# One front stage for vectors, modulation and column turns, and two expert slots filled during routing, in a one-core two-block network

## The reference

```python
mod = silu(c) @ w_mod + b_mod                    # c: one vector; shift, scale, gate for mixer and ffn
u   = rmsnorm(x, norm_mix_g) * (1 + sc_m) + sh_m      # 512 latent tokens
uc  = rmsnorm(ctx, norm_mix_g) * (1 + sc_c) + sh_c    # 256 context tokens, from silu(c_ctx) @ w_mod
y   = gated_deltanet(u, uc, w_in, conv_w, ...)        # projects u and uc first
...
aff = softmax(u2 @ w_router); gates, idx = top_k(aff.T, 64)   # 16 experts, 64 tokens each
hid = silu(xs @ w_gate) * (xs @ w_up); ys = hid @ w_down * gates   # 1024 -> 2048 -> 1024 per expert
```

## Time and profile before

| | us |
|---|---|
| median of 3 runs (lowest, highest) | 2763.99 (2762.11, 2767.11) |
| the profiled execution | 2771.04 |
| its span, first to last instruction | 2769.3 |
| front, start to the first instruction of `gdn_projection` | 74.46 |
| experts, first load issued to last piece landed | 930.5 to about 1898 |
| PE busy in the whole span | 2342.0 (85%) |

### The profile page before, as it was taken

How to read it: one execution, slowest core, us unless ns; L and a number is a source line. 1 busy time by engine, 2 the same in 40 slices (tenths; PEclk the granted TensorE clock), 3 DMA queues, 4 the chain that set the end, 5 groups by cost and what they waited for, 6 DMA issues and landing times. The chain is left out here.

```text
span 2769.3 us, 29918 instructions
## 1 busy us (share of the span) xinstructions
PE 2342.0 (85%) x11740; PEld 1515.1 (55%) x11740; DVE 1005.3 (36%) x1791; ACT 570.2 (21%) x1201; POOL 253.9 (9%) x347
## 2 busy tenths in 40 slices
PE   4999998189985688888888888885998989799998
PEld 2777668179944433333333333332775667687776
DVE  2576515525635101011010101103753554464443
ACT  2442214044401100000000000001232331223311
POOL 2233325820000000000000000000000000000000
PEclk7999988589996899999999999998998999899999
DMA  5123735334330599999999999994421022222030
GB/s 209 47 63 111 226 130 175 64 96 129 91 118 2 225 415 416 417 417 418 418 417 416 416 417 418 417 418 191 164 77 46 31 99 76 86 89 75 31 129 31
DMA packets 209191, 569.88 MB, mean 206 GB/s; under 512 B 62553, under 2 KB 97346, under 8 KB 175682
## 3 DMA queue, kind: packets, MB, share of 16 engines
q1 hardware_dynamic: 206296, 559.97, 53.3%
q0 software_dynamic: 2496, 8.40, 0.9%
q10 hardware_dynamic: 297, 0.11, 0.0%
HBM read 540.14 MB, written 28.31 MB: 205 GB/s over the span
## 5 line engine op out<-in xcount | busy, mean ns | idle before, releaser
L1808 PE MATMUL ps_gate_up<-expert_ring,one_expert_columns 128*64 128x512 f32 x1024 | 488.6, 635 | 143.7 <-DMA expert_ring<-in_moe_w_up_dram 136.2
L1809 PE MATMUL ps_gate_up<-expert_ring,one_expert_columns 128*64 128x512 f32 x1024 | 490.1, 636 | 0.0
L1808 PEld LDWEIGHTS ps_gate_up<-expert_ring,one_expert_columns 128*64 128x64 f32 x1024 | 144.6, 146 | 454.7 <-issue 454.7
L1875 DVE TENSOR_TENSOR hidden_tokens<-silu_gate,ps_gate_up 64x512 f32<-64x512 f32 x64 | 42.4, 690 | 623.3 <-ACT silu_gate L1854 622.8
L1788 PE MATMUL ps_down<-expert_ring,hidden_columns 128*64 128x512 f32 x512 | 226.6, 595 | 0.0
L1789 PE MATMUL ps_down<-expert_ring,hidden_columns 128*64 128x512 f32 x512 | 226.6, 595 | 0.0
L1809 PEld LDWEIGHTS ps_gate_up<-expert_ring,one_expert_columns 128*64 128x64 f32 x1024 | 144.6, 146 | 0.0
L1788 PEld LDWEIGHTS ps_down<-expert_ring,hidden_columns 128*64 128x64 f32 x512 | 67.5, 137 | 130.1 <-issue 127.9
L809 DVE SCALAR_TENSOR_TENSOR conv_out<-conv_in,tap_columns,conv_out 128x770 f32<-128x770 f32 (+1 forms) x96 | 124.4, 1295 | 3.4
L114 DVE TENSOR_TENSOR stream_low<-stream_raw,stream_high 128x2048 fp32r<-128x2048 f32 x48 | 110.0, 2293 | 1.6
L120 PE MATMUL even_bank<-stream_high,columns_high 128*128 128x512 f32 x256 | 107.7, 421 | 2.8 <-DVE columns_low L2377 2.8
(11 more groups left out here) (493 smaller groups left out, 4241.4 us busy)
## 6 DMA issues: line engine op xcount, KB each, us to landing
expert_ring<-in_moe_w_gate_dram SPq DMA_DIRECT2D x64, 2048.0 KB, 18.0
expert_ring<-in_moe_w_up_dram SPq DMA_DIRECT2D x64, 2048.0 KB, 22.5
expert_ring<-in_moe_w_down_dram SPq DMA_DIRECT2D x64, 2048.0 KB, 19.5
win_ring<-in_gdn_w_in_dram SPq DMA_DIRECT2D x16, 1024.0 KB, 6.7
late_mod_ring<-in_w_mod_dram SPq DMA_DIRECT2D x16, 1024.0 KB, 6.1
stream_raw<-in_w_in_even_dram SPq DMA_DIRECT2D x16, 1024.0 KB, 5.3
stream_raw<-in_w_in_odd_dram SPq DMA_DIRECT2D x16, 1024.0 KB, 5.2
stream_raw<-in_w_ple_gate_dram SPq DMA_DIRECT2D x8, 1024.0 KB, 5.0
```

Of the source, the lines that this page charges most:

```text
L1808: mm(psA[LO, c], xe[:, e, k], gu[:, s0, j, cols], start=(k == 0), stop=(k == KC - 1))
L1809: last = mm(psA[HI, c], xe[:, e, k], gu[:, s1, j, cols], start=(k == 0), stop=(k == KC - 1))
L1875: nc.vector.tensor_tensor(hid[HI, c % 2], sg[HI, c % 2], psA[HI, c], ALU.mult).then_inc(hidden, 1)
```

## The change

The four front blocks become one, `front`. SP issues the constants, the context, `x`, all four pieces of `w_mod` and the projection's first weights in one stream, each with its own semaphore. The tokens of context and latent are normalised in place and turned into columns without scale and shift, in two halves between PE's products with `w_mod`; ACT copies them plainly into one wide tile (`columns_wide`), and only when scale and shift are known does ACT apply them, SBUF to SBUF. DVE splits off the high part of all 768 columns and the low part of the latent 512; POOL takes the low part of the 256 context columns, a job that DVE had. In the experts, slots 0 and 1 of the ring are a tile of their own (`expert_ring_early`) that SP fills at the start of `route`; the load loop begins with piece 2, runs over 7 pairs and is followed by the 22 loads of the last pair. `gated` in `route` now lies over the normalised tokens, with a wait for their split into high and low.

```diff
+def front(nc, dram, per, U, spare, junk, loads):
...
+                sp.dma_start(per["ident_ones"][:, :, :], dram["gdn_const"][:, 0:2 * P].rearrange("p (a b) -> p a b", a=2)).then_inc(const_in, 16)
+                sp.dma_start(ctx[:, :, :], dram["ctx"].rearrange("b (t p) d -> p (b t) d", p=P)).then_inc(ctx_in, 16)
+                sp.dma_start(h[:, :, :], dram["x"].rearrange("b (t p) d -> p (b t) d", p=P)).then_inc(x_in, 16)
+                for i in range(PIECES):
+                    sp.dma_start(piece[i], w[:, :, i * COLS:(i + 1) * COLS]).then_inc(slot[i], 16)
+                sp.dma_start(per["gdn_const"][:, :], dram["gdn_const"]).then_inc(fetched, 16)
+                for dst, src in loads:
+                    sp.dma_start(dst, src).then_inc(fetched, 16)
+                sp.wait_ge(fetched, 16 * (len(loads) + 1))
...
+                for k in range(KC):
+                    pool.wait_ge(high, k + 1)
+                    nc.gpsimd.tensor_tensor(U[1][:, k, 0:CTX].bitcast(F32R), wide[:, k, 0:CTX], U[0][:, k, 0:CTX], ALU.subtract)
...
+                act.wait_ge(vec_kept, 2)
+                act.wait_ge(group_ready, 1)
                 c2 = cols[:, at["c"]:at["c"] + 2 * KC].rearrange("p (v k) -> p k v", v=2)
+                nc.scalar.activation(act_c[:, :, 0:2], c2, ACT.Silu).then_inc(c_ready, 1)
+                for t in range(NT):
+                    if t == 0:
+                        act.wait_ge(ctx_in, 16)
+                    if t == CT:
+                        act.wait_ge(x_in, 16)
+                    if t >= 2:
+                        act.wait_ge(squared, t - 1)
+                    nc.scalar.activation(junk[t % 2], tile[t].rearrange("p (a n) -> p a n", a=4), ACT.Square, accum_out=ss[:, 0, t:t + 1]).then_inc(squared, 1)
+                act.wait_ge(squared, NT)
+                nc.scalar.activation(ss[:, 1], ss[:, 0], ACT.Sqrt, scale=1.0 / D, bias=per["eps"][:, 0:1]).then_inc(rooted, 1)
+                for k in range(KC):
+                    act.wait_ge(turned, k + 1)
+                    nc.scalar.activation(wide[:, k, 0:CTX], psY[:, k % 2, 0:CTX], ACT.Copy)
+                    nc.scalar.activation(wide[:, k, CTX:N], psX[:, k % 2], ACT.Copy).then_inc(kept, 1)
                 rotary.on_scalar(act)
+                act.wait_ge(scales_ready, 2)
+                act.wait_ge(mod_ready, 2)
+                act.wait_ge(kept, KC)
+                for k in range(KC):
+                    for v, part in ((0, slice(0, CTX)), (1, slice(CTX, N))):
+                        last = nc.scalar.activation(wide[:, k, part], wide[:, k, part], ACT.Identity, scale=scale[v][:, k:k + 1],
+                                                    bias=bias[v][:, k:k + 1])
+                    last.then_inc(scaled, 1)
...
+                def turn_tokens(ks):
+                    pe.wait_ge(normed, NT)
+                    for k in ks:
+                        if k >= 2:
+                            pe.wait_ge(kept, k - 1)
+                        for t in range(CT):
+                            nc.tensor.transpose(psY[:, k % 2, t * P:(t + 1) * P], ctx[:, t, k * P:(k + 1) * P], ident)
+                        for t in range(LT):
+                            last = nc.tensor.transpose(psX[:, k % 2, t * P:(t + 1) * P], h[:, t, k * P:(k + 1) * P], ident)
+                        last.then_inc(turned, 1)
...
+                pe.wait_ge(c_ready, 1)
+                sum_piece(0)
+                turn_tokens(range(0, KC // 2))
+                sum_piece(1)
+                turn_piece(0)
+                turn_tokens(range(KC // 2, KC))
+                sum_piece(2)
+                turn_piece(1)
+                sum_piece(3)
+                turn_piece(2)
+                turn_piece(3)
...
+                dve.wait_ge(rooted, 1)
+                nc.vector.reciprocal(ss[:, 2], ss[:, 1]).then_inc(inverted, 1)
+                dve.wait_ge(inverted, 1)
+                for t in range(NT):
+                    nc.vector.tensor_scalar(tile[t], tile[t], ss[:, 2, t:t + 1], None, ALU.mult).then_inc(normed, 1)
+                for i in range(PIECES):
+                    move(i)
...
+                for k in range(KC + 1):
+                    if k < KC:
+                        dve.wait_ge(scaled, k + 1)
+                        take_high(nc, U[0][:, k], wide[:, k]).then_inc(high, 1)
+                    if k:
+                        dve.wait_ge(high, k)
+                        take_low(nc, U[1][:, k - 1, CTX:N], wide[:, k - 1, CTX:N], U[0][:, k - 1, CTX:N]).then_inc(low, 1)
...
+class EarlyPieces:
+    RING, EARLY, ROWS = 6, 2, 2
+    def __init__(self, m, dram):
+        self.ring = m.sb("expert_ring_early", [P, self.EARLY, self.ROWS * DFF])
+        self.slot = [m.sem(f"piece_loaded{i}") for i in range(self.RING)]
+        self.sources = [dram[n][0].rearrange("e (k p) f -> p e k f", p=P) for n in ("moe_w_gate", "moe_w_up")]
+    def load(self, sp):
+        for i in range(self.EARLY):
+            src = self.sources[i % 2][:, 0, i // 2 * self.ROWS:i // 2 * self.ROWS + self.ROWS, :]
+            sp.dma_start(self.ring[:, i].rearrange("p (k n) -> p k n", n=DFF), src).then_inc(self.slot[i], 16)
...
-        gated = m.sb("one_hot_gated", [P, LT, EXPERTS, CAP])
+        gated = xn[:, :, :].rearrange("p t (e c) -> p t e c", e=EXPERTS)
...
+            @block.sync
+            def _(sp):
+                early.load(sp)
...
+                dve.wait_ge(parted, 2)
...
+                def load(g, n):
+                    i, at = n % PIECES, g * 2 + n // PIECES
+                    ex = bass.ds(at, 1)
+                    if i < 2 * GROUPS_GU:
+                        src = (wg, wu)[i % 2][:, ex, i // 2 * ROWS:i // 2 * ROWS + ROWS, :].rearrange("p a k n -> p (a k) n")
+                    else:
+                        src = wd[:, ex, i - 2 * GROUPS_GU].rearrange("p a r d -> p (a r) d")
+                    if i < 2:
+                        sp.wait_ge(taken, at * GROUPS_GU + GROUPS_GU)
+                    elif i < RING:
+                        sp.wait_ge(downed, at * DOWN + (i - 2) + 1)
+                    else:
+                        sp.wait_ge(taken, at * GROUPS_GU + (i - RING) // 2 + 1 + GROUPS_GU)
+                    sp.wait_ge(downed, DOWN)
+                    if i == 2 * GROUPS_GU:
+                        sp.sem_inc(down_begun, 1)
+                    sp.dma_start((gu if i < 2 * GROUPS_GU else dn)[n % RING], src).then_inc(slot[n % RING], 16)
+                with sp.Fori(0, PAIRS - 1) as g:
+                    for n in range(EARLY, 2 * PIECES + EARLY):
+                        load(g, n)
+                for n in range(EARLY, 2 * PIECES):
+                    load(PAIRS - 1, n)
```

More of the change, by code:

```diff
@@ L274, in _ @@
             @block.scalar
             def _(act):
-                act.wait_ge(chain, 1)
-                c2 = cols[:, at["c"]:at["c"] + 2 * KC].rearrange("p (v k) -> p k v", v=2)
-                nc.scalar.activation(act_c[:, :, 0:2], c2, ACT.Silu).then_inc(act_ready, 1)
-                rotary.on_scalar(act)
+                for name, ap in per["vector_rows"]:
+                    n = ap.shape[0]
+                    act.dma_start(rows[at[name]:at[name] + n, :], ap).then_inc(rows_in, 16)
+                act.dma_start(taps[0:NTAP, :], dram["gdn_conv_w"].rearrange("a j (c p) -> (a j c) p", p=P)).then_inc(rows_in, 16)
@@ new lines, in turn_piece @@
+                def turn_piece(i):
+                    pe.wait_ge(moved, i + 1)
+                    for b in range(CB):
+                        last = nc.tensor.matmul(mod[:, i * CB + b, :], sums[:, i % 2, b * P:(b + 1) * P], group_sum[:, :],
+                                                start=True, stop=True)
+                    last.then_inc(in_columns, 1)
+                def turn_tokens(ks):
[8 more added lines that the diff above has]
+                        last.then_inc(turned, 1)
@@ L317, in _ @@
+                for i in range(PIECES):
+                    move(i)
                 dve.wait_ge(in_columns, PIECES)
[L318 removed]
+                b0 = at["b_mod"]
                 for v in range(2):
[L320 to L325 removed]
+                    nc.vector.tensor_tensor(modT[:, v, 0:2 * KC], mod[:, :, v], cols[:, b0:b0 + 2 * KC], ALU.add).then_inc(mod_ready, 1)
@@ L377, in finish_on_vector, with to_columns @@
                                          per["cols"][:, at:at + 4 * KC], ALU.add).then_inc(self.moved, 1)
-def to_columns(nc, per, tag, src, dst, norm, scale=None, bias=None, offset=0, keep=None, ahead=(), parts=None, at=0):
+def to_columns(nc, per, tag, src, dst, norm, scale=None, bias=None, offset=0, keep=None, ahead=()):
     nt = src.shape[1]
@@ L1581, in mixture_of_experts @@
             look("uT2", uT)
-            route(nc, per, uT, xn, wr, xsT, back, iota)
+            route(nc, per, uT, xn, wr, xsT, back, iota, early)
         look("xsT", xsT)
@@ L1703, in _, with experts @@
                     nc.vector.tensor_copy(back[:, n, :], psB[:, n % 2]).then_inc(bkept, 1)
```

(4 more changed lines are left out.)

218 lines of the change are left out of this document (74 added, 144 removed).

## The result

The changed kernel takes 2740.06 us (median of 4 runs, 2739.54 to 2743.18) against 2763.05 of the kernel before (4 runs, 2757.49 to 2767.11): ratio 0.9907, 95% interval 0.9892 to 0.9921, 23.0 us faster. Timed again on another chip it is 2738.42 against 2764.78, ratio 0.9901 (0.9885 to 0.9916). The forecast was 2740 in 2731 to 2750. The profiled execution took 2743.18, its span is 2741.4: 27.9 us less than the span of before.

A forecast was written before the change was run, and what follows sets the result against it. The front was taken as bound by a chain of waits, the experts by their transfers at 417 GB/s. Front 12 plus experts 11.6 gave 23.6 us off the median 2763.99: 2740, range 2731 to 2750 for eight in ten.

The forecast's parts named there:

- Experts, 11.6: Expert stage: two pieces fewer in the stream save 10.06 us, a first load 1.6 earlier the rest; 10.0 at least.
- Rival C: Experts: the early fill buys nothing, something other than transfers paces the stage; only the front counts, 2752 us; chance 0.06.
- Front, 12: Front: the projection starts at 61.8 us instead of 74.46, a gain of 12.7, rounded to 12; bounds 6.3 and 20.8.
- Now it waits for rows and identity: about 10.3: Start of the front: PE no longer waits for `x`, so its first turns come at about 10.3 us.
- I take the low level for the first 14 us of the chain: PE's chain in the front: low clock to 37.7 us, then 7.9 us at full clock, ending at 45.6.
- 1.75 per group: Scaling and splitting in the front: 0.5 + 0.6 + 0.65 us a group, 14.0 us for eight.
- Taking turns: Splitting in the front: DVE and POOL exclude each other on SBUF; without this the stretch would be 3.1 us less.
- Rival A: Front: PE's clock stays low through the whole chain; gain 6.3 + 11.6 = 17.9 us, 2746; chance 0.24.
- B: Front: full clock early and POOL working beside DVE; gain 20.8 + 11.6 = 32.4 us, 2732; chance 0.12.
- Rival D: Front: the rows starve behind SP's 14.3 MB and land at about 39 us; slower, 2775; chance 0.03.
- the rows stay at 10: Start of the front: engines go round the queues packet by packet, so SP's longer stream leaves the rows' landing at 10 us.
- if the stages in between change their length: Sign of a wrong prediction: the stages between front and experts change length; no size given.

The follow-up runs named there:

- e2: The kernel before with only the early fill of two expert slots added, its front unchanged; 2747.40 us against 2763.21, ratio 0.9947.
- e11: The changed kernel with one expert slot filled during the routing instead of two; one run, 2747.57 us.
- e5: The changed kernel with SP's expert loads behind the two early ones waiting for TensorE's first groups, as in the kernel before; one run, 2741.91 us.
- e8: The changed kernel with VectorE taking the whole low part, and `w_mod` and GpSimd's two small loads issued only after the rows landed; 2734.33 us, ratio 0.9885 to before.
- e3: The changed kernel with VectorE taking the low part of all 768 columns and GpSimd none; one run, 2745.94 us.
- e4: The changed kernel with SP asking for `w_mod` only when the row vectors have landed; one run, 2734.75 us.
- e7: The changed kernel with VectorE taking the whole low part and `w_mod` asked for only after the rows; 2728.91 us against 2764.97 before, ratio 0.9877.
- e1: The changed kernel's new front with the routing and experts of the kernel before; 2748.25 us against 2763.21 before, ratio 0.9942.
- e6: The changed kernel with GpSimd issuing its two small loads (positions, frequencies) only after the rows landed; one run, 2733.49 us.
- e9_changed_again: The changed kernel as it is, run for a second profile; one run, 2733.88 us.

## Why the prediction was right

**Experts, 11.6.** The stage went from 977.4 (two profiles) to 965.7 (nine), 11.6 us; the profile shown first has 968.0 and so only 10.1. The steps came as said: first load 1.8 earlier within the stage (said 1.6), TensorE 5.4 behind the memset (said 5.0), and no gap at the loop's return: the DMA share is 1.01 to 1.03 in every 20 us from 929 to 1849. Rival C is refuted by `e2` and `e11`. How the 11.6 splits is less sure than the total: the two pieces paid 5.8 and 4.8, 10.6 together against the 10.06 of the working, and the earlier start 1.1 against 1.6, from one profile each of `e11` and `e5`.

**Front, 12: the mechanism right, the size too small by 2.6 in this profile.** The start was said at 61.8 and came at 59.9; over six profiles of this front (those without an edit in it) the mean is 58.6. Three terms were mis-sized.
- "Now it waits for rows and identity: about 10.3" was 12.69 here and 11.7 to 12.7 over seven. The 10.0 of the earlier trace rows was one draw: in `e2`, with the same block as before, the rows' queue still moves 32 packets between 10 and 11 us and one between 11 and 12, and the first turn is at 13.58 instead of 12.60. GpSimd's loads and `w_mod` beside the rows probably add to it, since without both it is 10.34 (`e8`); how the 2.4 us divide between them and this scatter is not shown. The cost, 2.4 us, was carried through to the token turns (26.2 for 23.7).
- "I take the low level for the first 14 us of the chain" gave 21.9 for the chain; it was 5.7 us of low level (26.19 to 31.89) and 18.3 in all, 18.4 in one more profile, 17.3 to 17.4 in six, 16.2 in three. This is the largest error, 3.6, and it more than made up for the first.
- "1.75 per group" was 1.60, and the stretch to the projection 14.8 instead of 15.6.

**Taking turns** held and went further than the row I had argued from. The earlier trace rows showed it for an operation with two SBUF inputs; in this stage the cast, with one input, is held too (0.56 to 1.06). The Trainium skill (SBUF — State Buffer, section "SBUF: two separate sides") lists both kinds, operations with two SBUF inputs and those in a two-port mode, and has the pair of ports given to one engine for a whole instruction; the lengths of both kinds here agree, though the trace does not show in which mode the cast ran. `e3` puts the price at 1.7 us. Not giving GpSimd that work would have been right.

**Rival A** (low clock throughout) and **B** (full clock early, with both engines side by side) are both refuted: the clock rose after 5.7 us, and the stretched lengths show the two engines taking turns. B's full clock from the first token turn did come in `e4`, `e7` and `e8`. **Rival D** did not come, the rows do not starve: in the changed kernel their last packet comes between 12 and 12.6 us, while SP's stream goes on for some 30 us more. The Trainium skill (DMA: Bandwidth & Descriptors, section "Queues, rings and completion order") has the engines go round the queues packet by packet; the trace agrees in kind, since q10 moved packets all along. The prediction's step from that rule to "the rows stay at 10" failed: they came at 11.1 to 12.1 in seven profiles.

**The sum.** 23.6 was forecast and 23.0 measured (26.4 on the other chip); the profiled execution took 2743, where 2747 was expected. By stage the mean gains are 16.3 (74.9, the mean of before and `e2`, to 58.6) and 11.6, 27.9 in all, so 1.5 to 5 us are missing from the medians. With the front's term 4 us too small and the medians' sum right, part of the agreement to the microsecond is luck. The prediction named one sign of being wrong that did show, "if the stages in between change their length": the projection is 3.4 shorter in this profile, the recurrence 2.8. The projection moves by 5.6 between two profiles of the changed kernel, and the recurrence by 8.0 between those of before and `e2`, which have the same code there, so the sign could not tell a wrong prediction from a right one. Routing is 1.6 longer in this profile than in that of before. The first 18.3 us of the gather, before and changed (columns as in the earlier trace rows):

```profile
889.70:908.00 18.30, 18.23 (x73) 14.75 (x74) 4.55 (x5) 6.23 (x8) 0.00 (x0) 0.92 0.00 0
```

```profile
868.60:886.90 18.30, 18.11 (x66) 14.54 (x67) 4.67 (x5) 5.58 (x8) 0.00 (x0) 0.83 0.00 0
```

The granted clock is 0.83 instead of 0.92, and TensorE gets through 66 instructions instead of 73. The difference, 0.09 of 18.3 us, is the 1.6. No transfer runs in either window, so the early loads do not slow the gather as it runs. Routing takes 73.9 in the second profile of the same kernel. Of the ten profiles with both halves, six have 75.4 or 75.5, two 73.9 and two 72.3 or 72.4; those of before, `e1` and `e2` have 73.9. Whether the change makes the longer case commoner, or shifts something else between stages, stays open; no run here tells.

## What to carry to other kernels

Where a stage is bound by a steady stream of transfers, count the bytes that can be moved before it: the two 2.1 MB pieces paid 5.8 and 4.8 us here, the first although the consumer could not begin with it alone. Before giving a second engine a share of elementwise work, look for a row in which both work on SBUF at once; a share that makes the first engine's other instruction wait costs more than it takes off. And when several loads move to the program's start, look at what lands beside the smallest and most urgent one: with a 2 KB load on another queue and the megabytes not needed yet both held back, the first turn came at 10.3 instead of 11.7 to 12.7, in one profile.

## What the runs showed of the hardware

- A load of 2 KB issued by GpSimd (16 packets of 128 bytes on q0) took up to 1.44 us a packet in the changed kernel. From 6 to 8 us q0 held 44 to 51% of the DMA engines' time for 0.01 MB in the nine profiles that have this load there, and SP's queue moved 0.34 to 0.43 MB instead of 0.77 to 0.79 in the two where it was held back. Held back, the same load took less in one profile (2.5 us over all 16 packets in `e6`, 16.1 in the changed kernel) and not much less in the other (12.0 in `e8`). The view counts a packet where it starts, so a window that leaves out the start of these long packets shows idle engines that are not idle.
- TensorE's clock around the pause between its first product and the token turns: in the three profiles with pauses of 0.97, 1.81 and 1.82 us every token turn ran at the full level (four in 0.60); in the eight with pauses of 2.20 to 3.57 some or all of the first half ran at the low one (1.06). These eight are not alike: in three (the changed kernel, `e3`, `e6`) the record's first rise comes only at 31.89, 31.15 and 28.36, in the other five it rose between 21.7 and 23.6 and fell again between 25.1 and 27.0. No run varies the pause alone, so this is an order seen in eleven profiles and no rule.
- The granted clock of a window can be 1.00 only because nothing was recorded. In the changed kernel's profile the clock record begins at 31.89 with the rise to full, and the view counts the time ahead of it as full speed: it says 1.00 for 26 to 31.5 us, while turns take 1.06. In `e9_changed_again` the record begins at 22.13, and its 0.73 agrees with the lengths: low until 28.96 (turns of 1.06), full behind it (0.60 from 29.49). Ahead of the record's first change, the lengths are what can be read. The changed kernel's window, then that of `e9_changed_again`:

```profile
26.00:31.50 5.50, 5.31 (x25) 4.82 (x25) 0.73 (x2) 2.62 (x6) 3.53 (x11) 1.00 1.04 386
```

```profile
26.00:31.50 5.50, 5.50 (x39) 4.05 (x37) 0.01 (x1) 3.39 (x8) 2.53 (x9) 0.73 1.04 387
```
